# Modulation panels in column groups, a fourth place for attention weights, and output projections that begin inside the attentions

## The reference

```
mod = jax.nn.silu(c) @ ada_w[l] + ada_b[l]          # c is 1 x 1024, ada_w[l] 1024 x 6144
sh_m, sc_m, g_m, sh_f, sc_f, g_f = jnp.split(mod, 6, axis=-1)
hn = adaln(x, mix_norm_g[l], sh_m, sc_m)            # norm times (1 + scale), plus shift
... = jnp.split(hn @ w_in[l], IN_SPLITS, axis=-1)
o_a = diff_attention(...)                           # and o_b latent, o_c indexed, o_d band attention
y = jnp.concatenate([o_a, o_b, o_c, o_d], axis=-1) @ w_out[l]
x = x + g_m[:, None, :] * y
hn = adaln(x, ffn_norm_g[l], sh_f, sc_f)
f = swiglu(hn, ...)   # l = 0;  moe_swiglu, eight experts, for l = 1
x = x + g_f[:, None, :] * f
```

## Time and profile before

| what | value |
|---|---|
| median of 3 runs | 2692.15 us |
| profiled execution, own time | 2694.97 us |
| its span | 2693.2 us |
| PE busy | 2578.2 us, 96% |
| DVE, ACT, POOL busy | 1726.7, 1306.3, 301.1 us |
| mean granted clock | 0.982 |
| transfers | 627.29 MB, 233 GB/s |

### The profile page before, as it was taken

One profiled execution on the slowest core, in us unless ns is written; L12 is line 12 of the kernel. 1 busy time (PEld: TensorE's weight loads), 2 busy tenths in 40 slices (PEclk: granted clock), 3 DMA queues, 4 the chain that ended last, 5 costly groups with the idle time before them and its releaser, 6 DMA issues.

```text
span 2693.2 us, 39037 instructions
## 1 busy us (share of the span) xinstructions
PE 2578.2 (96%) x13620; PEld 2139.9 (79%) x13620; DVE 1726.7 (64%) x2535; ACT 1306.3 (49%) x1931; POOL 301.1 (11%) x288
## 2 busy tenths in 40 slices
PE   7899999999899999989999988999999999999998
PEld 7677899887487998767998766888888888887886
DVE  1312777663225773465553464989898988889897
ACT  2211544421123442243331243777777777777775
POOL 0465000870270000000000000000000000000000
PEclk9999999999899999999999998999999999999999
DMA  8345544442355444315444313989898989899897
GB/s 321 125 179 213 208 185 168 177 174 92 110 219 198 190 183 179 110 48 195 183 183 174 107 58 135 377 320 383 325 379 323 370 329 378 335 346 355 341 355 285
DMA packets 87635, 627.29 MB, mean 233 GB/s; under 512 B 9760, under 2 KB 9920, under 8 KB 12800
## 3 DMA queue, kind: packets, MB, share of 16 engines
q1 hardware_dynamic: 84512, 613.45, 60.1%
...
...
## 4 chain that ended last, share of the span: by engine, by line
PE 92%; DVE 4%; ACT 2%; issue 1%; POOL 1%; DMA 0%; DVEq 0%; SPq 0%; ACTq 0%; POOLq 0%
PE bank L994 23%; PE bank L885 14%; PE bank L1022 11%; PE bank L605 11%; PE bank L899 7%; PE bank L618 6%; PE bank L838 6%; PE bank L1122 1%; PE bank L1083 1%; PE bank L964 1%; PE bank L1037 1%; PE bank L1009 1%; PE bank L677 1%; PE bank L693 1%; PE bank L664 1%
## 5 line engine op out<-in xcount | busy, mean ns | idle before, releaser
L1457 ACT ACTIVATE sb_parts<-sb_ring 128x1024 fp32r<-128x1024 f32 x873 | 872.9, 1053 | 125.4 <-PE bank L1022 38.9
L2222 DVE TENSOR_TENSOR sb_parts<-sb_ring,sb_parts 128x1024 fp32r<-128x1024 f32 x675 | 786.4, 1217 | 10.8 <-ACT sb_parts L1457 10.8
L994 PE MATMUL bank<-sb_parts 128*128 128x512 f32 x2688 | 661.4, 396 | 2.5 <-DVE sb_parts L2214 1.8
L994 PEld LDWEIGHTS bank<-sb_parts 128*128 128x128 f32 x2688 | 495.0, 188 | 113.3 <-issue 9.4
L885 PE MATMUL bank<-sb_parts 128*128 128x256 f32 x3168 | 387.1, 284 | 7.1 <-DVE sb_XT L2147 5.8
L885 PEld LDWEIGHTS bank<-sb_parts 128*128 128x128 f32 x3168 | 385.9, 193 | 9.9 <-issue 7.7
L1022 PE MATMUL bank<-sb_parts 128*128 128x512 f32 x1344 | 323.9, 390 | 0.0
L1022 PEld LDWEIGHTS bank<-sb_parts 128*128 128x128 f32 x1344 | 251.7, 188 | 52.1
L1457 ACT ACTIVATE sb_REG<-bank 128x512 f32<-128x512 f32 (+2 forms) x119 | 67.9, 576 | 408.3 <-PE bank L605 211.4
L605 PE MATMUL bank<-sb_XT,sb_ring 128*128 128x256 f32 x1152 | 257.5, 384 | 6.9 <-DVE sb_XT L1969 3.9
L2124 DVE TENSOR_TENSOR sb_parts<-sb_ring,sb_parts 128x1024 fp32r<-128x1024 f32 x198 | 232.8, 1219 | 34.3 <-ACT sb_parts L1457 34.3
...
## 6 DMA issues: line engine op xcount, KB each, us to landing
...
```

The costliest lines, as they stand in the source:

```text
L994: m = nc.tensor.matmul(banks[par][:, :], x[:, k, :], w[:, cols], start=k == 0 and t == 0, stop=k == KD - 1 and t == 2, skip_group_check=True)
L1457: return nc.scalar.activation(out, in_, ACT.Copy)
L2222: V_.tensor_tensor(LOW[u], ring[slot][:, 1024 * c:1024 * c + 1024], HIGH[u], ALU.subtract) \
```

## The change

It does three things.

1. All 48 panels are multiplied on PE, two panels (a "pair") at a time. For row block k the stationary operand is the condition's column broadcast to 32 columns, and it goes to column group k mod 4, so 16 matmuls 128x256 (L559) leave four partial rows, each 32 times, in one bank of 128 x 512. ACT copies the bank to `PARTIAL` (four places), and a `take` on PE sums its 128 partitions, which gives the result times 32; DVE multiplies by 1/32 and adds the bias. There are twelve hooks of two pairs: in the last steps of moba, before the transposes of xat0, ffn0, mix1, xat1, ffn1, mix2, ffn2, mix3 and ffn3, one pair in each of levels 2 and 3 of mix1, and before the outputs of the delta rule. GpSimd no longer touches panels.
2. `PR` has four places. ACT makes the exponentials of unit s before it copies the turned weights of unit s - 2, and gives DVE's and its own copies other steps (LATE 5 to 6 and 6 to 8, TURN_AT 8 to 10, a pooling panel from unit 1 to 2). The squares for the differential norm stand on ACT after the whole attention.
3. `OUT_AT`: a part of the output projection is issued in the last steps of the attentions: in moba half of the first panel (banks 0 and 1 of four), in s0 and s1 half of panel 0 at step 8, the other half and half of panel 1 at step 10, the rest of panel 1 at step 11. `project` does what is left.

```diff
-        PR = r.tile(3, 2, T)
+        PR = r.tile(4, 2, T)
...
+        OUT_AT = {"moba": {4: ((0, (2, 3)),)}}
+        OUT_AT["s0"] = OUT_AT["s1"] = {8: ((0, (0, 1)),), 10: ((0, (2, 3)), (1, (0, 1))), 11: ((1, (2, 3)),)}
...
-        ADA_AT = {"xat0": 1, "ffn0": 1, "mix1": 1, "xat1": 1, "ffn1": 1, "mix2": 4,
-                  "ffn2": 3, "mix3": 3, "ffn3": 2}
...
+        ADA_PAIRS = {h: (2 * i, 2 * i + 1) for i, h in enumerate(
+            ("moba", "xat0", "ffn0", "mix1", "levels", "delta", "xat1", "ffn1", "mix2", "ffn2", "mix3", "ffn3"))}
+        TAKE_AFTER = {"xat0": {("xq", 1): 0, ("xq", 3): 1, ("xk", 0): 2, ("xk", 1): 3},
+                      "xat1": {("xq", 0): 10, ("xq", 1): 11, ("xq", 2): 12, ("xq", 3): 13}}
...
-        LATE = {0: "d_q", 1: "d_k", 3: "d_v", 4: "c_q", 5: "c_k", 6: "c_v"}
-        LATENT_AT, ROPE_AT, TURN_AT = 2, 3, 8
+        LATE = {0: "d_q", 1: "d_k", 3: "d_v", 4: "c_q", 6: "c_k", 8: "c_v"}
+        LATENT_AT, ROPE_AT, TURN_AT = 2, 3, 10
...
+            def ada(hook, in_banks=(4, 5)):
+
+                pe.wait_ge(sem("silu_cond"), 1)
+                for x, i in enumerate(ADA_PAIRS[hook] if isinstance(hook, str) else hook):
+                    ps = claim(("ada", i), in_banks[x]) if in_banks else claim_aside(("ada", i))
+                    used = []
+                    for half in range(2):
+                        ada_panels[state["panel"]] = ADA_ORDER[2 * i + half]
+                        pn, slot = panel()
+                        used.append(pn)
+                        wt = cols_of(slot)
+                        for k in range(KD):
+                            g = 32 * (k % 4)
+                            m = nc.tensor.matmul(ps[g:g + 32, half * T:half * T + T],
+                                                 sm("cond", 8)[:, k:k + 1].broadcast_to([P, 32]), wt[:, k, :],
+                                                 start=k < 4, stop=k >= 4, skip_group_check=True)
+                    filled(m, ("ada", i))
+                    for pn in used:
+                        release(pn, ("ada", i))
...
             def transpose_norm(n):
 
-                ada(n, ADA_AT.get(n, 0))
+                if n in ADA_PAIRS:
+                    ada(n)
                 pe.wait_ge(sem("xhat_ready"), 2 * (TURNED.index(n) + 1))
...
+                    if key == "moba" and q == len(us) // 2:
+                        ada("moba", (6, 7))
+                    for rp, js in OUT_AT[key].get(q, ()):
+                        out_part(name, rp, js, **out)
...
+            ada("delta")
             pe.wait_ge(sem("delta_out"), 1)
...
+            def partials(hook):
+
+                for i in ADA_PAIRS[hook] if isinstance(hook, str) else hook:
+                    wait_full(act, ("ada", i))
+                    if i >= 4:
+                        wait_full(act, ("taken", i - 4))
+                    read_out(copy(PARTIAL[:, i % 4, :], bank_of(("ada", i))[:, :]), ("ada", i))
...
                 attention(k2)
+                wait_drained(act, ("mixed", k2, 0))
+                nc.scalar.activation(DSQ, OT[:, 0:2, :], ACT.Square).then_inc(sem("diff_squares"), 1)
...
-                        m = V_.tensor_tensor(dst, ps, dst, ALU.add)
+                        m = V_.scalar_tensor_tensor(dst, ps, 1.0 / 32, dst, ALU.mult, ALU.add)
```

321 lines of the change are left out of this document (126 added, 195 removed).

## The result

The changed kernel takes 2699.31 us (median of 20 runs, 2693.68 to 2702.01); the kernel before took 2694.05 in the same session (20 runs, 2689.85 to 2697.25). The ratio is 1.0019 with a 95% interval of 1.0012 to 1.0025: 5 us slower. The profiled execution of the changed kernel took 2701.35 us, with a span of 2699.6.

A forecast was written before the change was run, and what follows sets the result against it. TensorE, busy 96% of the span, bounds the kernel, with its waits and lower-clock stretches. The stage terms sum to +9.1 us on a median of 2692.15, giving 2701 us; the range leaving 2 in 10 out is 2683 to 2714.

The forecast's parts named there:

- The pair in four groups at once: On PE, 16 matmuls of two panels in four column groups: 2.0 us a pair, 4.0 a hook.
- Rival 1: Only two column groups run at a time on PE: 3.6 us a pair, +5.7, 2707 us; chance 0.13.
- The serial case: Column groups on PE don't overlap: 6.9 us a pair, hooks of 13.8, +68, 2769 us; chance 0.03.
- Norms held before ffn0 and ffn1: ACT's squares wait until T + 6.4, T being the last projection matmul's end; transposes at T + 10.7: +7.5 each.
- the step on gate 0: Before the feed-forwards: gate 0 lands at T + 1.35, its low half ends T + 3.6, DVE's additions only then.
- The norm before ffn2: Residual at T + 8.7 behind gate 0's low half, transposes at T + 13.0: +2.8, and 1.2 for clock, +4.0.
- xat0: Waits for a key panel, GpSimd's sum and DVE go (6.3), takes -1.7, hook +0.5: -7.5.
- mix0: moba's last steps: two pairs and half a projection panel, 7.45, cover 6.2 of PE's waits: -2.2.
- mix1 and delta: Two pairs in busy levels, +3.8 with the norm; delta's hook fills PE's wait and keeps the clock, -3.0.
- mix2, mix3: Norms: shorter hooks -3.15 and -2.8, clock +2.5 and +0.8, takes +3.2 and +2.9, gate takes +1.6 and +0.6.
- s0, s1: Projection pieces in waits -3.5, earlier exponentials and turn -2.0, late squares +1.6, later turn +0.8: -3.1 each.
- the five norm terms: Norms before ffn0 and ffn1 (+7.5 each), mix2 (+4.1), ffn2 (+4.0) and mix3 (+1.5).

The follow-up runs named there:

- groups64: Changed kernel with two column groups of 64 columns in place of four of 32; 2703.19 us, 1.0041 of the kernel before.
- one_group: Changed kernel with all eight row blocks in one column group of 32; 2779.89 us, one run.
- norm_first: Changed kernel with the norm's ACT and DVE work ahead of gate 0's and up 0's halves before ffn0, ffn1, ffn2; 2687.64 us, 0.9984 of the kernel before.
- moba_out_after: Changed kernel with OUT_AT empty for moba only, the half projection panel back behind the attention; 2696.25 us, 1.0009 of the kernel before.
- part1_alone: Changed kernel with parts two and three undone, only the panels on PE in column groups kept; 2704.75 us, 1.0042 of the kernel before.
- act_order: Changed kernel with ACT's exponentials again behind the copy of the turned weights of the unit two back; 2721.10 us, 1.0103 of the kernel before.
- levels_moved: norm_dsq with the levels' two pairs moved to later hooks, four pairs before mix2, two takes out of the levels; 2672.32 us, 0.9917 of the kernel before.
- s_out_after: Changed kernel with OUT_AT empty in s0 and s1, the whole projection behind the attention there; 2706.53 us, 1.0047 of the kernel before.
- norm_dsq: norm_first with the differential norm's squares on ACT directly behind their copy again; 2681.15 us, 0.9954 of the kernel before.

## Why the prediction was right, and where not

The forecast was 2701 us, slower, with 9.1 us to the kernel before; measured are 2699.3 and 5. Its likeliest case, the norms held before ffn0 and ffn1, is the one that holds. That the total is so near is in part luck: the terms miss by more, both ways.

- **The pair in four groups at once** (2.0): 1.83, and the three kernels with other groups show that it is the groups side by side. Rival 1 was a real kernel, groups64: 3.57 a pair as its 3.6 said, and 6 us more, as its 5.7 said. The serial case, one_group, is 80 us more where 68 stood.
- **Norms held before ffn0 and ffn1** (+7.5 each): +5.3 and +5.6, shown by norm_first. PE's transposes were put at T + 10.7 and are at T + 10.0, with 1.3 for the clock (3.30 for 1.97) where 1.9 was said. What failed is the step on gate 0: "gate 0 waits for the third projection panel (T - 3.45)". It does wait for it, but a projection panel is 6.9 us (the prediction itself has 3.45 for half of one, under mix0), so that panel ends at T - 6.9. The additions, put at T + 6.4, ended at T + 2.6 and held nothing; the squares waited for up 0 on ACT, to T + 5.7.
- **The norm before ffn2** (+4.0): +0.3. This term rested wholly on the same step, since there the residual's longer chain (0.69 four times and 2.29) was put behind gate 0's low half. Without it the residual ends at T + 3.0, as before, and only up 0 is late, which puts the squares at T + 5.8 instead of T + 3.1. PE's transposes come 10.1 us after T, where three panels had held them until T + 10.2 before.
- **xat0** (-7.5): -8.7, the waits for the key panel and for GpSimd gone as said. The row for two scalings "alone" (78.33) was misread: GpSimd was at work then too, with another operation (L2758 at 76.60 and 78.82), so GpSimd's work does not slow DVE in every case. In s0, where GpSimd is silent, the same two take 0.62 as well (1120.32), so 0.62 against 2.52 stands as the comparison.
- **mix0** (-2.2): -5.0. Of the waits I counted 6.2 us as covered by 7.45 of work; all but 0.83 of the last four went, and the earlier one of 1.73 is 0.60. A term is missing, the clock: before lost 2.9 us to it behind those waits (106 to 114), the changed kernel nothing. The half panel of the projection had no part in it, as moba_out_after shows (75.27 us for 75.46). The pairs alone take the last four (part1_alone has the same single 0.83), but the stage is 78.14 us there: 2.3 of the 5.0 come with part one, near the forecast. The other 2.7 come with part two, of which no term of the prediction speaks here: in part1_alone the wait of 1.72 is still there, with a drop of the clock behind it. They are not ACT's order, since act_order has 75.46 too; the fourth place and the pooling panel that moved from unit 1 to 2 are left, and no run tells them apart.
- **mix1 and delta** (+0.8): +9.4 in the profiled execution, and +2.8 to +5.6 in the profiles of eight other kernels whose code is the same from ffn0's first product to there. Two terms are mis-sized. For the norm of mix1 up to the recurrence +3.8 was said, and it is +7.5 here, +4.2 to +5.9 in the eight (without the norm +6.3, and +4.4 to +6.0); levels_moved shows what was worth taking out there, two pairs (3.7) and two takes (1.6). From the recurrence to the end of the projection -3.0 was said; it is -0.3 to -2.6 in the eight and +1.7 here. That execution lost the clock in the recurrence (37.5 us to the turned outputs, 33.4 to 33.7 in the eight). No other execution shows the same: one_group's 41.4 are its hook of 15.26 us, which starts at 724.17, and its clock held until 723. Why it fell so early is open: before, the same small matmuls ran at full clock until 676.
- **mix2, mix3** (+4.1, +1.5): +1.4, +0.6. DVE's gate takes ahead of the index sum cost PE 3.40 in place of 2.08 before the values (L615 waits for ACT's copy), as said; the clock terms of 2.5 and 0.8 were too high, since before lost as much in the same stage (4.9 us at 1054 to 1064 and 1092 to 1098, after 5.0 in three places).
- **s0, s1** (-3.1 each): -1.9, -1.8. The pieces, put at 7.0 in both together, are worth 7.5 us by the medians (s_out_after, 3 to 12), and 3.3 by place, since they leave L759's wait for the squares open. The squares were put at 3.2 for both and are 4.3 by place in norm_dsq.

So the total is closer than its terms: mix1, s0, s1 and the rest cost 12.2 us more than said in that execution, the five norm terms 11.4 less, and mix0, xat0, xat1 and ffn3 gained 5.6 more. With the 1.8 before moba, where it is scatter, that is the 6.4 of the profiled execution but for rounding.
